# TensorE kept busy from the program's begin, one input piece on another queue, a third split sub-tile, and a new table of priority offsets

## The chip, the cores and the metric

One Trainium2 chip, eight cores, all running the same program on their own share of the data: core c works on half a stream of the prompt group (2048 rows of 1024 numbers) and on two short running streams (32 rows in all). TensorE is the matmul engine, VectorE (DVE), ScalarE (ACT) and GpSimd (POOL) do the element-wise work, and SyncE (SP), ScalarE and GpSimd each have a queue on which transfers are issued. The metric is the device time in microseconds (us) of one launch, taken from its slowest core.

## The reference

```python
def encoder_layer(x, ...):
    xn = rmsnorm(x, g_mix_pre)
    proj = xn @ w_in                       # 1024 -> 2048: [u | B | C | h]
    ...                                    # y_pool: trailing means of u, y_conv: gated conv of width 3
    merged = concat([group_rmsnorm(y_pool, ...), group_rmsnorm(y_conv, ...)])
    x = x + rmsnorm(merged @ w_out, g_mix_post)
    x = x + rmsnorm(cross_attn(rmsnorm(x, g_x_pre), mem_k, mem_v, w_q, w_co), g_x_post)
    hid = square(relu(rmsnorm(x, g_ff_pre) @ w_up))      # 1024 -> 4096
    x = x + rmsnorm(hid @ w_down, g_ff_post)
```

Three sub-layers, then: a mixer, attention into 256 memory rows, and an MLP with weights of 1024 x 4096. Each core also computes a share of the memory's keys and values, and the states that the streams carry on.

## The kernel before

The 2048 rows are four tiles of 512, each of four sub-tiles of 128 rows. `xT` holds a tile turned (features on partitions), `win`, `wout`, `up` and `wdn` hold weights as bf16, converted while they are loaded over GpSimd's queue. The stages run one after the other: the mixer of tiles 0 to 3, attention of tiles 2, 3, 0, 1, the MLP of tiles 0 to 3. Between the stages a tile goes to memory (`x1`, `x2`) and comes back.

The code only records operations, each with its engine, what it reads and writes, and an estimated cost. `Prog.schedule` then plays the program through with these estimates, and at each step an engine takes the ready operation with the lowest `prio`. What comes out is a fixed sequence per engine; in the run every engine executes its own in that order and waits with semaphores. `prio` is the place at which an operation was recorded, less an offset that the table `ORDER` gives for a named part and an engine. All matmuls have one line in the profile (L716), as do transposes (L721), ACT activations (L745) and transfers (L790).

The begin: tile 0 comes as four pieces `XT[0]` to `XT[3]` of 512 KB each, already turned, all on SP's queue. `pre_first` takes piece after piece: a square on ScalarE, two `scale_rows` that write `xT`, a sum on VectorE; the sum over partitions is one float32 matmul on `onesf`. ScalarE issues the load of `cst`, and then its first activation `warm`; the loads of w_in on GpSimd's queue wait for `warm` (`after=warm`). Behind them stand the rows of tile 1 and then w_out, one transfer of 4 MB read from memory, of which the first matmul `ps<-wout,mg` needs all.

`out_tile(t, ...)` is the product that closes a stage: per sub-tile two banks of PSUM (a pair) take nk chunks in two halves of 512 columns, and `post` then normalizes and adds. With `late=True` (MLP, tile 0) the first half of the chunks is done for two sub-tiles before the second half of `wdn` is asked for. There are four pairs in all.

Of the kernel before, what the change touches and what calls it, by code (L numbers as in the profile page):

```python
# [8 lines left out]
BF16 = mybir.dt.bfloat16  # L9
# [9 lines left out]
TN = 512  # L19
# [171 lines left out]
class Op:  # L191
# [2 lines left out]


ORDER = {
    ("conv_group 0", "dve"): -180, ("conv_group 12", "dve"): -70, ("conv_group 13", "act"): 340, ("conv_group 15", "dve"): 250,
    ("conv_group 6", "act"): -130, ("conv_group 7", "dve"): -50, ("ext_state_out 0", "pe"): -120, ("fin_conv 0", "dve"): -120,
# [6 lines left out]
    ("pool_group 14", "act"): 90, ("pool_group 6", "dve"): 60, ("post 10", "act"): 350, ("post 8", "dve"): -60,  # L205
    ("pre_sub 11", "act"): -30, ("pre_sub 12", "dve"): -10, ("pre_sub 13", "pe"): -120, ("pre_sub 2", "act"): 190,
# [4 lines left out]
}  # L211


class Prog:
# [72 lines left out]
    def schedule(self):  # L287
# [14 lines left out]
            if op.ndep == 0:  # L302
                release(op)

        free = {e: 2.0 if e == "pool" else 1.0 for e in self.ENGS}
        hold = {e: 0.0 for e in self.ENGS}
        bank_free = [0.0] * 8
        bank_busy = [None] * 8
# [70 lines left out]
        while left or any(dq.values()):  # L379
# [19 lines left out]
            now, e = best  # L399
# [21 lines left out]
            o, bk = pick  # L421
# [142 lines left out]
def build_program():  # L564
    nc = bass.Bass("TRN2", target_bir_lowering=False)
    BASE.clear()
    P = Prog(nc, n_dma_sems={"sp": 40, "pool": 24, "act": 4})
# [218 lines left out]
    def memset(ap, v, eng="dve"):  # L786
        P.add([(eng, lambda e, L: e.memset(ap, v), 0.3)], writes=[ap])
# [31 lines left out]
    warm = act(stat(128), epsb[:, 0:1], AF.Square)  # L819
    copy(idb[:, :], idf[:, :])  # L820

    def load_consts():
        memset(ones[:, :], 1.0)
        memset(onesf[:, :], 1.0)
        memset(onesr[:, :].bitcast(F32), 1.0)
        memset(bd64[:, :], 0.0)
        memset(bd64[0:64, 0:64], 1.0)
        memset(bd64[64:128, 64:128], 1.0)
        tt(pg[:, :], pv[:, 0:4], pv[:, 16:20], ALU.mult)

    def load_wpool():
        load(wpool[:, :], wpool_d[:, :], 262144, q="pool", after=warm)
# [106 lines left out]
    @named("pre_first")  # L939
    def pre_first():  # L940

        for i in range(4):
            x = XT[i]
            v = sqx[min(i, 1)][:, :]
            act(v, x, AF.Square)
            for c in range(2):
                kc = 2 * i + c
                scale_rows(xT[0][:, kc * TN:(kc + 1) * TN], x[:, c * TN:(c + 1) * TN], gcs[:, kc:kc + 1])
            if i > 0:
                tt(sqx[0][:, :], sqx[0][:, :], v, ALU.add)  # L950
        q = sqx[0][:, 0:TN]
        tt(q, q, sqx[0][:, TN:2 * TN], ALU.add)
        ps = PS(1)
        o2 = ps.v(0, 128, 0, TN)
        P.add([("pe", lambda e, L: e.matmul(L(o2), lhsT=onesf[:, :], rhs=q, start=True, stop=True, skip_group_check=True), 0.95)],
              reads=[onesf[:, :], q], writes=[o2])
        ln = rf[0][:, :]
        act(ln, o2, AF.Ln, scale=1.0 / D, bias=epsb[:, 0:1])
        act(r0[:, :], ln, AF.Exp, scale=-0.5)
        act(r0sq[:, :], ln, AF.Exp, scale=-1.0)  # L960

    def out_tile(t, chunks, nk, w, gp, dst, late=False):
# [10 lines left out]
                mm(ps.v(0, 128, h * 512, (h + 1) * 512), chunks(kc)[:, i * 128:(i + 1) * 128], w(kc, h),  # L973
                   kc == 0, kc == nk - 1)
        if late:
            for i in range(2):
                part(i, 0, nk // 2)
        for i in range(NSUB):
            part(i, nk // 2 if late and i < 2 else 0, nk)
            ps = tiles[i]  # L980
            X = Xof[(t, i)]
            row = t * TN + i * 128
            if dst is yp and t == NT - 1 and i == NSUB - 1:
                post_halves(ps, X, gp, yp[row:row + 128, :])
                continue
            post(ps, X, 128, gp, free_se=late_stage[0])
            if dst is None:
                continue
            dma("sp", dst[row:row + 128, :], X, 524288, wr=(dst is not yp))
# [494 lines left out]

    load_win(0, warm)
    for i in range(4):
        load(XT[i], xt0[i], 524288)
    load_consts()
    load_win(1, warm)
    load(Xe[0:NX, :], xe[:, :], NX * 4096, q="pool", after=warm)  # L1490
    load_wpool()
# [258 lines left out]
```

How the kernel before makes its waits and increments, by code:

```python
        def run(e, eng):  # L503
            seen = {}
            ends = sorted(dma_last.items(), key=lambda kv: kv[1].end)
            for n, op in enumerate(seqs[e]):
                if e == "sp" and n == len(seqs[e]) - 1:
                    for k, last in ends:
                        if last.end < op.start - SETTLED and seen.get(k, 0) < last.semval:
                            eng.wait_ge(dsem[k], last.semval)
                            seen[k] = last.semval
                waits = {}
                for p in plan[op]:
                    k, v = (p.sem, p.semval) if p.is_dma else (p.eng, p.sigval)
                    if seen.get(k, 0) >= v:
                        continue
                    if waits.get(k, 0) < v:
                        waits[k] = v
                for k, v in waits.items():
                    eng.wait_ge(dsem[k] if isinstance(k, tuple) else esem[k], v)
                    seen[k] = v
                ins = op.fn(eng, lambda x: x.resolve(psum) if isinstance(x, PV) else x)
                if op.is_dma:
                    ins.then_inc(dsem[op.sem], 16)
                elif op.needs_signal:
                    ins.then_inc(esem[e], 1)
            if e == "sp":
                for k, last in ends:
                    if seen.get(k, 0) < last.semval:
                        eng.wait_ge(dsem[k], last.semval)
```

## Time and profile before

| | |
|---|---|
| median of three runs | 840.95 us |
| fastest of them | 839.43 us |
| the profiled execution | 839.23 us |
| its span on the slowest core (core 3) | 837.7 us |
| spans of the eight cores | 834.6 to 837.7 us |
| TensorE busy in the span | 809.7 us (97%), 4529 matmuls |
| VectorE, ScalarE, GpSimd busy | 396.7, 386.4, 105.2 us |
| read from memory | 146.48 MB |

The span runs from the first to the last instruction of a core; 1.5 us of the profiled execution lie around it. A matmul of 512 columns is shown as 379 ns long at full clock, but its successor starts about 216 ns after it, since matmuls are pipelined.

### The profile page before, as it was taken

Reading aid. Unit: us, or ns where it says so; the run is one execution under the profiler, and the core shown is the slowest. Engines: PE = TensorE matmul, PEld = TensorE weight load, DVE = VectorE, ACT = ScalarE, POOL = GpSimd, SP = SyncE. Lnnn points to the kernel's source line nnn. Section 1 sums busy time; section 2 is a strip of 40 time slices with the busy share of each in tenths; the row PEclk is TensorE's granted clock in tenths of the full one; section 3 lists DMA queues with packets and bytes.
Section 4 is the critical chain, followed back from the end, with each engine's and each line's share of the span. In section 5 each row is a group of like instructions: output and inputs, shape, how many; then the busy total and the mean of one; then the engine's idle time right before and its main releaser. Section 6 shows DMA issues by size and latency. Waiting matters only on the chain.

```text
span 837.7 us, 13527 instructions; the slowest of 8 cores (834.6 to 837.7 us)
## 1 busy us (share of the span) xinstructions
PE 809.7 (97%) x4529; PEld 386.3 (46%) x4529; DVE 396.7 (47%) x552; ACT 386.4 (46%) x801; POOL 105.2 (13%) x182
## 2 busy tenths in 40 slices
PE   2889999999999999999999999999999999999997
PEld 1444445444564455454444454454444444444443
DVE  4797867689786676574231222232132322222112
ACT  4588756848775757674340323332133401233101
POOL 7523202130111104110010000000000000000000
PEclk9999999999999999999999999999999999999999
DMA  8999499430496526985799527861258810194011
GB/s 188 184 232 209 110 240 229 86 59 1 68 153 110 202 79 174 160 149 117 133 163 168 150 88 144 154 124 51 101 118 153 156 52 26 54 163 86 6 46 51
DMA packets 27120, 103.43 MB, mean 123 GB/s; under 512 B 2402, under 2 KB 9186, under 8 KB 21292
## 3 DMA queue, kind: packets, MB, share of 16 engines
q0 software_dynamic: 16736, 68.37, 47.4%
q1 hardware_dynamic: 10028, 33.80, 11.8%
q8 instruction: 38, 0.62, 0.3%
q10 hardware_dynamic: 288, 0.39, 0.2%
q14 instruction: 30, 0.25, 0.1%
HBM read 146.48 MB, written 18.07 MB: 196 GB/s over the span
## 4 chain that ended last, share of the span: by engine, by line
PE 85%; DMA 11%; issue 1%; POOL 1%; DVE 1%; ACT 1%; DVEq 0%; POOLq 0%; ACTq 0%
PE ps L716 83%; DMA wout<-w_out 6%; DMA wdn<-w_down 4%; PE ps L721 2%; DMA up<-w_up 1%; POOL win L790 0%; DVE mg L771 0%; DVE X L771 0%; POOL wdn L790 0%; DVE V L752 0%; ACT L745 0%; POOL X L790 0%; DVE xT L752 0%; POOL sT L790 0%; DVE z L752 0%
## 5 line engine op out<-in xcount | busy, mean ns | idle before, releaser
L716 PE MATMUL ps<-wdn,hid 128*128 128x512 bf16 x1024 | 222.3, 379 | 1.0 <-DMA wdn<-w_down 1.0
L716 PE MATMUL ps<-xT,up 128*128 128x512 bf16 x1024 | 222.8, 379 | 0.0
L716 PEld LDWEIGHTS ps<-wdn,hid 128*128 128x128 bf16 x1024 | 99.9, 98 | 120.5 <-issue 1.4
L716 PEld LDWEIGHTS ps<-xT,up 128*128 128x128 bf16 x1024 | 99.6, 98 | 119.6 <-issue 1.1
L752 DVE TENSOR_TENSOR O<-ps,gp 128x1024 f32<-128x1024 f32 (+1 forms) x49 | 58.7, 1200 | 184.5 <-PE ps L716 124.1
L745 ACT ACTIVATE rt<-ps 128x512 bf16<-128x512 f32 x128 | 76.4, 597 | 139.3 <-PE ps L716 133.3
L716 PE MATMUL ps<-xT,win 128*128 128x512 bf16 x512 | 124.4, 385 | 15.3 <-DMA win<-w_in 15.3
L752 DVE TENSOR_TENSOR hid<-rt 128x512 bf16<-128x512 bf16 x128 | 54.4, 425 | 150.8 <-ACT rt L745 148.9
L745 ACT ACTIVATE sqj<-ps 128x1024 bf16<-128x1024 f32 (+1 forms) x33 | 32.8, 994 | 175.8 <-PE ps L716 174.0
L716 PEld LDWEIGHTS ps<-xT,win 128*128 128x128 bf16 x512 | 49.9, 99 | 74.1 <-issue 19.2
L771 DVE SCALAR_TENSOR_TENSOR X<-O,st,X 128x1024 f32<-128x1024 f32 (+1 forms) x49 | 62.3, 1277 | 6.0 <-DVE O L752 5.4
L790 POOL DMA_DIRECT2D up<-w_up x32 | 17.2, 538 | 376.7 <-PE ps L716 357.6
L716 PE MATMUL ps<-wout,mg 128*128 128x512 bf16 x256 | 62.8, 379 | 0.8 <-DMA wout<-w_out 0.8
L716 PE MATMUL ps<-xT,Am 128*128 128x512 bf16 x256 | 58.2, 379 | 0.0
L716 PE MATMUL ps<-Bm,mg 128*128 128x512 bf16 x256 | 57.5, 379 | 0.0
L745 ACT ACTIVATE xs<-X 128x1024 bf16<-128x1024 f32 x40 | 42.1, 1053 | 32.9 <-DMA X<-x 25.0
L752 DVE TENSOR_TENSOR xT<-ps,cst 128x1024 bf16<-128x1024 bf16 x40 | 48.2, 1220 | 18.5 <-PE ps L721 18.4
L716 PEld LDWEIGHTS ps<-wout,mg 128*128 128x128 bf16 x256 | 24.8, 98 | 28.8 <-issue 1.6
L716 PEld LDWEIGHTS ps<-Bm,mg 128*128 128x128 bf16 x256 | 24.3, 98 | 28.4 <-issue 1.0
L716 PEld LDWEIGHTS ps<-xT,Am 128*128 128x128 bf16 x256 | 24.1, 98 | 28.3 <-issue 1.8
L754 POOL TENSOR_TENSOR psm<-mg 128x512 fp32r<-128x512 bf16 x16 | 19.2, 1198 | 94.8 <-ACT st L745 46.6
L745 ACT ACTIVATE rf<-ps,epsb 128x512 f32<-128x512 f32 x33 | 22.5, 682 | 15.6 <-PE ps L716 9.6
(203 smaller groups left out, 700.1 us busy)
## 6 DMA issues: line engine op xcount, KB each, us to landing
up<-w_up POOLq DMA_DIRECT2D x32, 1024.0 KB, 9.4
x<-X SPq DMA_DIRECT2D x16, 512.0 KB, 4.2
X<-x SPq DMA_DIRECT2D x16, 512.0 KB, 3.9
wdn<-w_down POOLq DMA_DIRECT2D x8, 1024.0 KB, 30.1
yp<-X SPq DMA_DIRECT2D x15, 512.0 KB, 2.6
X<-xp POOLq DMA_DIRECT2D x8, 512.0 KB, 44.0
X<-xp SPq DMA_DIRECT2D x8, 512.0 KB, 5.4
win<-w_in POOLq DMA_DIRECT2D x4, 768.0 KB, 25.5
```

The lines of the kernel that those rows point to most:

```text
L716: P.add([("pe", lambda e, L: e.matmul(L(out), lhsT=lhsT, rhs=rhs, start=start, stop=stop, skip_group_check=True), max(0.03, n * 0.000421 + ...
L721: P.add([("pe", lambda e, L: e.transpose(out=L(out), in_=in_, identity=idn), 0.065 if in_.dtype == BF16 else 0.25)], reads=[in_, idn], wri ...
L745: return e.activation(out=L(out), in_=L(in_), func=func, scale=scale, **kw)
L752: opts.append(("dve", lambda e, L: e.tensor_tensor(out=L(out), in0=L(in0), in1=L(in1), op=op), c_dve(n, per)))
L754: opts.append(("pool", lambda e, L: e.tensor_tensor(out=L(out), in0=L(in0), in1=L(in1), op=op), 0.18 + n * 0.00168))
L771: return P.add([("dve", lambda e, L: e.scalar_tensor_tensor(out=L(out), in0=L(in0), scalar=scalar, in1=L(in1), op0=op0, op1=op1), c_dve(nc ...
L790: return P.add([(q, lambda e, L: e.dma_start(out=out, in_=in_), 0.5 + nbytes / desc * 0.0005 if q == "pool" else 0.43)], reads=[in_] if rd ...
```

## The change

It has four parts. TensorE gets 34 matmuls whose result nobody reads (`spin`): 16 on a tile of ones, which need nothing but a memset, and 6 each after the first three pieces of tile 0 have been scaled. Piece 3 of tile 0 is loaded over ScalarE's queue, and the pieces are taken in the order 0, 3, 1, 2. The MLP's `out_tile` for tile 0 does the first half of three sub-tiles ahead, not of two. And `ORDER` has 67 offsets in place of 57, most of them other ones; with it the planner takes GpSimd to be free at 2.8, not 2.0.

```diff
@@ ORDER: all lines replaced; two of each
-    ("conv_group 0", "dve"): -180, ("conv_group 12", "dve"): -70, ("conv_group 13", "act"): 340, ("conv_group 15", "dve"): 250,
-    ("kv_block 0", "pe"): 40, ("kv_block 1", "act"): -280, ("kv_block 1", "pe"): -250, ("kv_block 3", "pe"): -60,
...
+    ("attn_head 1", "pe"): 620, ("attn_head 13", "pe"): 130, ("attn_head 14", "pe"): -250, ("conv_group 0", "dve"): -180,
+    ("group_rstd 7", "pe"): -30, ("kv_block 1", "pe"): -250, ("kv_block 3", "pe"): -60, ("out0_ 2", "pe"): -110,
...
-        free = {e: 2.0 if e == "pool" else 1.0 for e in self.ENGS}
+        free = {e: 2.8 if e == "pool" else 1.0 for e in self.ENGS}
...
+    busy = at("busy", hids.off + 2048, TN, BF16)
...
+        memset(busy[:, :], 1.0)
...
+    def spin(rhs, n, half):
+
+        o = PS(1).v(0, 128, 0, TN)
+        for _ in range(n):
+            P.add([("pe", lambda e, L: e.matmul(L(o), lhsT=ones[:, :], rhs=rhs, start=True, stop=True, skip_group_check=True),
+                    0.427 if half else 0.2133)], reads=[ones[:, :], rhs], writes=[o], lead=10 ** 6)
...
-        for i in range(4):
+        for j, i in enumerate((0, 3, 1, 2)):
             x = XT[i]
-            v = sqx[min(i, 1)][:, :]
+            v = sqx[min(j, 1)][:, :]
...
+            if j < 3:
+                spin(xT[0][:, 2 * i * TN:(2 * i + 1) * TN], 6, False)
...
         if late:
-            for i in range(2):
+            for i in range(3):
                 part(i, 0, nk // 2)
         for i in range(NSUB):
-            part(i, nk // 2 if late and i < 2 else 0, nk)
+            part(i, nk // 2 if late and i < 3 else 0, nk)
...
     for i in range(4):
-        load(XT[i], xt0[i], 524288)
+        load(XT[i], xt0[i], 524288, q="act" if i == 3 else "sp")
     load_consts()
+    spin(busy[:, :], 16, True)
```

ScalarE's sequence now opens with two transfers, `cst` and the piece, and then `warm`. Lines of the kernel's helpers move down a little: L716 becomes L718, L721 becomes L723.

What stands in a row, at three places. The first is TensorE's sequence around the first product with w_out (`wout,mg_80`: tile 0); `xs` are rows of tile 1 about to be turned, `xT_54` is tile 0 and `xT_55` tile 1. Before:

```order
L716 MATMUL ps<-xT_54,win 128x512 x24
L721 MATMUL ps<-idb,xs_59 128x128 x8
L721 MATMUL ps<-idb,xs_58 128x128 x8
L716 MATMUL ps<-sqe,bd_48 128x128
L721 MATMUL ps<-idb,xs_59 128x128 x8
L716 MATMUL ps<-wout,mg_80 128x512
L716 MATMUL ps<-sq_106,bd_48 128x512
L716 MATMUL ps<-wout,mg_80 128x512 x11
```

317 matmuls stand ahead of that first product. With the change:

```order
L718 MATMUL ps<-xT_54,win 128x512 x14
L718 MATMUL ps<-sqe,bd_48 128x128
L723 MATMUL ps<-idb,xs_59 128x128 x8
L723 MATMUL ps<-idb,xs_58 128x128 x8
L718 MATMUL ps<-wout,mg_80 128x512 x8
L718 MATMUL ps<-sq_106,bd_48 128x512
L718 MATMUL ps<-wout,mg_80 128x512 x7
L718 MATMUL ps<-xT_55,win 128x512 x23
```

351 matmuls stand ahead of it now, the same 317 in another order and the 34 of `spin`.

The second place is TensorE's sequence in the middle of the first stage, where rows of tile 2 (`xs0_58`, its second sub-tile) are turned between the products of tile 1 with w_out and of the memory with w_k. Before:

```order
L716 MATMUL ps1<-wout_91,mg1_81 128x512 x2
L716 MATMUL ps0<-wkv1_114,mT0_110 128x512
L716 MATMUL ps1<-wout_91,mg1_81 128x512
L716 MATMUL ps0<-wkv1_114,mT0_110 128x512
L716 MATMUL ps1<-wout_91,mg1_81 128x512
L721 MATMUL ps3<-idb_44,xs0_58 128x128 x8
L716 MATMUL ps0<-wkv1_114,mT0_110 128x512
```

With the change:

```order
L718 MATMUL ps0<-wout_91,mg1_81 128x512
L718 MATMUL ps3<-wkv1_114,mT0_110 128x512
L718 MATMUL ps0<-wout_91,mg1_81 128x512 x2
L723 MATMUL ps3<-idb_44,xs0_58 128x128 x8
L718 MATMUL ps0<-wout_91,mg1_81 128x512
L718 MATMUL ps2<-wkv1_114,mT0_110 128x512
```

660 matmuls stood ahead of these transposes, now it is 648 without those of `spin`. These rows come into the buffer that tile 0's second sub-tile leaves; its last w_out matmul was number 541, and is now number 506.

The third place is TensorE's sequence at the end of the MLP of tile 0: `wdn0` to `wdn3` are the first half of w_down, `wdn4` to `wdn7` the second. Before:

```order
L716 MATMUL ps2<-wdn2_142,hid1_132 128x512 x8
L716 MATMUL ps2<-wdn3_143,hid1_132 128x512 x8
L716 MATMUL ps1<-wdn4_144,hid2_133 128x512 x8
L716 MATMUL ps1<-wdn5_145,hid2_133 128x512 x8
L716 MATMUL ps1<-wdn6_146,hid3_134 128x512 x8
```

With the change:

```order
L718 MATMUL ps2<-wdn3_143,hid1_132 128x512 x8
L718 MATMUL ps1<-wdn0_140,hid0_131 128x512 x8
L718 MATMUL ps1<-wdn1_141,hid0_131 128x512 x8
L718 MATMUL ps1<-wdn2_142,hid1_132 128x512 x8
L718 MATMUL ps1<-wdn3_143,hid1_132 128x512 x8
L718 MATMUL ps0<-wdn4_144,hid2_133 128x512 x8
```

The 32 matmuls of the third sub-tile's first half have moved ahead of the first one that reads `wdn4`; the rest of the MLP keeps its order.

## Rows read from the trace of the kernel before

**Rows 1.** Cores 1, 3 and 7: span and mean granted TensorE clock.

```profile
core 1: 837.3 us, clock 0.999
...
core 3: 837.7 us, clock 0.999
...
core 7: 837.3 us, clock 1.000
```

**Rows 2.** Core 3 by stage: window, its length, busy time (instructions) of each engine, granted clock, DMA share, GB/s.

```profile
0.00:15.00 15.00, 0.00 (x0) 0.00 (x0) 5.87 (x16) 5.27 (x6) 11.52 (x26) 1.00 0.80 183
15.00:62.00 47.00, 42.20 (x322) 20.84 (x323) 37.83 (x78) 32.04 (x74) 18.82 (x43) 1.00 1.02 206
62.00:435.00 373.00, 371.35 (x2195) 181.61 (x2193) 253.73 (x310) 243.60 (x508) 63.27 (x92) 1.00 0.66 136
435.00:832.00 397.00, 396.05 (x2018) 183.86 (x2015) 97.13 (x146) 104.26 (x210) 11.64 (x22) 1.00 0.48 100
```

**Rows 3.** Core 3, who TensorE waited for: us in total, times, longest.

```profile
PE ps L716 <- DMA win<-w_in: 15.3, 1, 15.3
PE ps L716 <- ACT sq L745: 1.1, 2, 0.9
```

**Rows 4.** Core 3, TensorE in order of time, the first matmuls.

```profile
15.30 6.38 PE L716 MATMUL ps<-xT,win 128*128 128x512 bf16 x16 [15.30 <-DMA win<-w_in]
...
23.35 1.04 PE L716 MATMUL ps<-xT,win 128*128 128x512 bf16 x4
```

**Rows 5.** Core 3, the chain that ended last, in order of time.

```profile
11.73 49.27 DMA wout<-w_out
...
424.78 31.79 DMA wdn<-w_down
```

**Rows 6.** TensorE just before and at the first w_out matmul: cores 3, 1 and 7.

```profile
59.86 0.61 PE L721 MATMUL ps<-idb,xs 128*128 128x128 bf16 x8 [0.89 <-ACT xs L762]
61.24 0.38 PE L716 MATMUL ps<-wout,mg 128*128 128x512 bf16 x1 [0.77 <-DMA wout<-w_out]
...
60.95 0.38 PE L716 MATMUL ps<-wout,mg 128*128 128x512 bf16 x1 [1.17 <-DMA wout<-w_out]
...
60.70 0.38 PE L716 MATMUL ps<-wout,mg 128*128 128x512 bf16 x1
```

**Rows 7.** Core 3, the start of the DMAs: timeline, then DMA share and GB/s in windows.

```profile
1.07 0.41 ACTq L790 DMA_DIRECT2D cst<-consts  x1
...
2.87 0.20 ACT L745 ACTIVATE st<-epsb 128x1 f32<-128x1 f32 x1
3.68 1.21 POOL L790 DMA_DIRECT2D win<-w_in  x2 [2.98 <-ACT st L745]
...
5.00:6.00 1.00, 0.00 (x0) 0.00 (x0) 0.00 (x0) 0.00 (x0) 1.00 (x3) 1.00 0.65 128
6.00:7.00 1.00, 0.00 (x0) 0.00 (x0) 0.00 (x0) 0.00 (x0) 1.00 (x2) 1.00 0.86 199
```

**Rows 8.** Core 3, the second tile-2 transposes: the reload, the scaling, the matmuls.

```profile
120.92 1.06 ACT L745 ACTIVATE xs<-X 128x1024 bf16<-128x1024 f32 x1 [1.70 <-DMA X<-xp]
...
123.75 1.13 ACT L762 ACTIVATE xs<-X,st 128x1024 bf16<-128x1024 f32 x1
...
125.14 0.61 PE L721 MATMUL ps<-idb,xs 128*128 128x128 bf16 x8 [0.72 <-ACT st L745]
```

**Rows 9.** Core 3, around the matmuls on dg.

```profile
167.61 2.75 POOL L754 TENSOR_TENSOR dg<-idb,rb 128x1536 bf16<-128x1536 bf16 x1 [0.90 <-DVE rb L781]
167.97 2.93 DVE L771 SCALAR_TENSOR_TENSOR mg<-z,cst,rf 128x512 bf16<-128x512 f32 x1
...
171.65 0.81 PE L716 MATMUL ps<-dg,ones 128*128 128x512 bf16 x3 [0.73 <-DVE V L752]
```

**Rows 10.** TensorE at the second half of w_down: cores 3 and 7.

```profile
456.71 18.51 PE L716 MATMUL ps<-wdn,hid 128*128 128x512 bf16 x85 [0.95 <-DMA wdn<-w_down]
...
456.33 3.83 PE L716 MATMUL ps<-wdn,hid 128*128 128x512 bf16 x17 [1.24 <-DMA wdn<-w_down]
```

More of the change, by code:

```diff
@@ L196 @@
 ORDER = {
-    ("conv_group 0", "dve"): -180, ("conv_group 12", "dve"): -70, ("conv_group 13", "act"): 340, ("conv_group 15", "dve"): 250,
-    ("conv_group 6", "act"): -130, ("conv_group 7", "dve"): -50, ("ext_state_out 0", "pe"): -120, ("fin_conv 0", "dve"): -120,
[6 rows of a table removed]
-    ("pool_group 14", "act"): 90, ("pool_group 6", "dve"): 60, ("post 10", "act"): 350, ("post 8", "dve"): -60,
-    ("pre_sub 11", "act"): -30, ("pre_sub 12", "dve"): -10, ("pre_sub 13", "pe"): -120, ("pre_sub 2", "act"): 190,
[4 rows of a table removed]
+    ("attn_head 1", "pe"): 620, ("attn_head 13", "pe"): 130, ("attn_head 14", "pe"): -250, ("conv_group 0", "dve"): -180,
+    ("conv_group 1", "dve"): 30, ("conv_group 10", "act"): -170, ("conv_group 12", "dve"): 410, ("conv_group 4", "dve"): 60,
+    ("conv_group 6", "act"): 60, ("ext_conv 3", "dve"): 40, ("fin_attn 0", "pe"): -30, ("fin_attn 1", "act"): 60,
+    ("fin_attn 1", "pe"): 120, ("fin_attn 10", "act"): 180, ("fin_attn 11", "pe"): 60, ("fin_attn 12", "pe"): -110,
+    ("fin_attn 5", "act"): 50, ("fin_conv 0", "dve"): -240, ("fin_conv 1", "act"): -150, ("fin_conv 3", "act"): 240,
[5 rows of a table added]
+    ("pool_group 3", "dve"): -190, ("post 0", "act"): 460, ("post 0", "dve"): 460, ("pre_sub 1", "act"): 240,
[5 rows of a table added]
 }
@@ L948, in pre_first @@
                 scale_rows(xT[0][:, kc * TN:(kc + 1) * TN], x[:, c * TN:(c + 1) * TN], gcs[:, kc:kc + 1])
-            if i > 0:
+            if j < 3:
+                spin(xT[0][:, 2 * i * TN:(2 * i + 1) * TN], 6, False)
+            if j > 0:
                 tt(sqx[0][:, :], sqx[0][:, :], v, ALU.add)
```

18 rows, old and new, of the table ORDER are left out of this document.

## The prediction

> **What bounds the kernel now.** I read the cores first: the odd ones are the slow ones, 837.3 to 837.7 us, at a granted clock of 0.999 [rows 1]. Core 3, the slowest, carries the sum. Then the stages: TensorE is idle for 15.0 us until its first matmul, for 47.00 - 42.20 = 4.8 us until 62 us, for 373.00 - 371.35 = 1.65 us until 435 us and for 0.95 us until 832 us [rows 2]; then come the last normalization and store. From 62 us on it is the bound and nearly gap-free, so only its idle time and matmuls at half pace can be won. The waits put names to the first part: w_in 15.3 us, and 1.1 us for squares of ScalarE [rows 3].
>
> At the begin 16 matmuls take 6.38 us, some 400 ns from one to the next, and four later ones 1.04 us, some 217 ns apart [rows 4]; both spacings are 512 columns, at 1.2 and at 2.4 GHz. Before the first of them TensorE had done nothing. Less the last one's own 0.38 us, 15 steps took 6.0 us; at 216 ns they take 3.24. The half pace cost 2.8 us. That is what `spin` is about.
>
> The view that decides is the chain: from 11.73 us on, 49.27 us of it are the transfer of w_out, to 61.00 us [rows 5], and at 61.24 us TensorE, idle for 0.77 us, starts its first product with it; on core 1 it waited 1.17 us, on core 7 not at all [rows 6]. Meanwhile the DMA engines have no free time (share 1.02 from 15 to 62 us [rows 2]). Up to 61 us this program is bound by bytes, with TensorE just behind.
>
> **Part 1: the spin matmuls.** 16 start when `ones` and `busy` are set, about 2 us into the span, and even at 1.2 GHz they need 16 x 0.427 = 6.8 us: done by 9, six before the 15.3 us at which real work begins. The other 18 wait for scaled pieces and take 18 x 0.216 = 3.9 us at full pace; only those behind the third piece could delay anything, and w_in and the fourth piece are later. So they cost nothing on the path, the cover being the 15 us of waiting; without cover they would cost 10.7 us. Worth: up to 2.8 us by TensorE's clock. One extra memset on VectorE lies ahead of any data.
>
> **Part 2: piece 3 on ScalarE's queue.** It can start real work earlier. From 5 to 7 us the DMA engines stood at 0.65 and 0.86 [rows 7]: 0.35 + 0.14 = 0.5 us of transfer that a second queue can fill. It also has a price. ScalarE now issues two transfers ahead of `warm`, which ran at 2.87 us, and GpSimd's first load waits for `warm` until 3.68 us [rows 7]. One more issue like the first (0.41 us [rows 7]) moves all of GpSimd's queue by as much, w_out with it. So w_out lands between 0.5 us earlier and 0.4 us later; I take 0.1 us earlier.
>
> The Trainium skill's page "DMA: Bandwidth & Descriptors", under "Queues, rings and completion order", states that SP's and ScalarE's queues are rings on the same 16 DMA engines, which take turns between rings. By that rule the piece gets a larger share against GpSimd's loads, and no byte ahead of w_out disappears; the share of 1.02 agrees, and the sum stays as it is.
>
> **Parts 1 and 2 together, where it counts.** The order shows the same 317 real matmuls ahead of the first w_out product as before. If TensorE reaches this point 3 us or more earlier, it waits there for w_out: no other work has been put in front. So of 2.8 us and an earlier begin, what counts on core 3 is the 0.77 us of present wait plus the 0.1 us: 0.87 at the landing itself. But the last transposes before it waited 0.89 us for ScalarE's scaled rows [rows 6], and a part of what is behind w_out comes from the same queue of ScalarE; core 7, which did not wait for w_out, can gain less still. TensorE does not start at once when the transfer lands either (61.00 to 61.24). Ends: 1.3 us gained, 0.4 us lost. I take 0.5 us.
>
> **Part 3: the new order from 62 to 435 us.** In this stretch of core 3 there are 1.65 us of idle to win [rows 2], of which two waits are 0.72 us [rows 8] and 0.73 us [rows 9]. The first is TensorE waiting for rows of tile 2 that ScalarE had begun to square only at 120.92 us, after 1.70 us of waiting for their reload. With the change tile 0's second sub-tile finishes 541 - 506 = 35 matmuls earlier, some 35 x 0.216 = 7.6 us or less (transposes among them are shorter), and frees the buffer by as much; the transposes stand only 12 matmuls (2.6 us) earlier. This wait should go: 0.72 us. In the second, a VectorE operation took 2.93 us while GpSimd built `dg` in 2.75 us [rows 9]. GpSimd still builds `dg` just there, so VectorE is held up again; four matmuls of tile 2 now stand behind the `dg` matmuls and not ahead of them, which helps nothing. I leave that wait. New waits of the size of those present, one or two of 0.7 to 0.9 us, are as likely as anywhere in a new order. Ends: 1.65 us gained, 1.8 us lost. I take 0.6 us.
>
> **Part 4: the third split sub-tile.** TensorE waits 0.95 us for the second half of w_down, 1.24 us on core 7 [rows 10]; the transfers take 31.79 us from an issue that follows TensorE's own progress [rows 5], so an earlier or later TensorE brings the same wait. Now 32 matmuls, 32 x 0.216 = 6.9 us, are put ahead of it. They read weights and rows that are long there, and their pair of PSUM is free, since the fourth sub-tile, the small products and the next tile use the pairs in the same rhythm. The wait is covered seven times. The posts of the first two sub-tiles come 6.9 us later, to no harm: TensorE then has tile 1's products ahead of it for over 60 us. Worth 0.95 us, between 0.76 and 1.24 by core.
>
> **Sum.** 839.23 - 0.5 - 0.6 - 0.95 = 837.2 us, against the profiled execution. The median of the runs shown lies 1.7 us above that execution, the fastest 0.2 us; I go between: **838.0 us**.
>
> **Rivals.** First, **the begin passes through.** If w_out landed some microseconds earlier too, or its transfer were not what holds all cores, the 2.8 us of half pace and about 1.5 us of earlier begin would stay, with 0.6 and 0.95 us as above: 839.23 - 5.85 = 833.4 us, some 834 as a median. For it speaks core 7, where TensorE did not wait for w_out [rows 6]. Against it: there too the product began at 60.70 us, and the bytes ahead are the same. Chance 0.12.
>
> Second, **the second transposes of tile 2 wait longer.** They stand 12 matmuls earlier. If their rows came no earlier than now (reload landed at about 120.9 us, scaled by 124.88 us [rows 8]), TensorE would wait 0.72 + 2.6 = 3.3 us there in place of 0.72. The point that decides is whether the store and reload of that buffer go out with the earlier sub-tile or stay queued on SP behind another store. Then 839.23 - 0.5 - 0.95 + 2.6 = 840.4 us in the execution, 841.2 as a median, a little slower than before. Chance 0.15.
>
> Third, **nothing but w_down**: w_out lands 0.4 us later, the order's gains and losses cancel; 839.23 + 0.4 - 0.95 = 838.7 us, 839.5 as a median. Chance 0.2.
>
> Fourth, **a limiter on the clock.** In the rows the cores are granted 0.999 or 1.000 [rows 1] while all eight run dense matmuls; were TensorE's 809.7 busy us granted 13/16 instead, they would take 997 us. The Trainium skill, in "TensorE: Matmul & The Clock Gate" under "Seeing it yourself", states such a step to 13/16 once three cores of a die run dense matmuls, and that operands of ones don't trip it. By it the kernel before would have to show it already, and the trace disagrees. Chance 0.01.
>
> **How the numbers follow.** The forecast has 0.52. Its own bounds are 839.23 - 1.3 - 1.65 - 1.24 = 835.0 and 839.23 + 0.4 + 1.8 - 0.76 = 840.7 in the execution. The range must leave out no more than 2 in 10: down to 834.5, which cuts off most of the first rival, up to 841.5, which takes in the second and third. 2% of 841 us are 17 us, about what a measurement of this kernel can tell from no change; no case but the limiter comes near it, and idle time that could be won is about 15 us at the begin, which is bytes. Faster by over 2%: 0.01, slower: 0.01, within: 0.98.
>
> **What would show it.** In the changed kernel's profile the first matmuls should stand at about 2 us, and the first 16 on `win` some 216 ns apart (about 3.6 us together). TensorE should then wait for w_out for 2 us or more, landing at 60.5 to 61.4 us on core 3. The wait for w_down should be gone on all cores, that for tile 2's second sub-tile too, and the one at `dg` should remain. Wrong would be the forecast if w_out's wait stayed under 1 us with its product well before 60 us, or if a wait of over 1.5 us appeared between 62 and 435 us.

## The result, and the profile of the changed kernel

The changed kernel takes **846.51 us** (median of six executions, 846.16 to 847.87); the kernel before, timed beside it on the same chip, 841.56 us. The ratio is **1.0065, 95% interval 1.0046 to 1.0085**: 5.5 us slower (3.9 to 7.2), where 838.0 us, some 3 us faster, was forecast. Within 2% it is the same, as the chances had it; its sign and its size were wrong, and 846.5 lies outside the range of 834.5 to 841.5. The ratios here and below leave out executions in which the cores of one die ran slow at a lower granted clock (one of the kernel before took 1002.69 us at 0.816); medians beside them don't, so I go by ratios.

The profiled execution took 847.87 us. The cores first, as in [rows 1]: these are 4.3 to 8.6 us longer than before, and the fastest of the eight (841.6) is longer than the slowest was (837.7), so the loss is not that of one core.

```profile
core 1: 841.6 us, clock 0.999
...
core 3: 846.3 us, clock 0.995
...
core 7: 844.7 us, clock 0.996
```

The same stages of core 3 as in [rows 2]:

```profile
0.00:15.00 15.00, 9.48 (x30) 3.50 (x31) 5.47 (x18) 5.23 (x6) 11.04 (x24) 0.89 0.82 181
15.00:62.00 47.00, 41.46 (x333) 20.84 (x332) 40.16 (x80) 30.82 (x73) 22.05 (x47) 1.00 1.02 206
62.00:435.00 373.00, 369.51 (x2114) 177.94 (x2113) 252.06 (x308) 237.05 (x497) 64.32 (x90) 1.00 0.64 131
435.00:832.00 397.00, 397.00 (x2053) 184.89 (x2052) 99.07 (x152) 106.83 (x213) 12.58 (x24) 1.00 0.50 103
```

Read the instruction counts, not the busy time. From 62 to 435 us TensorE is idle for 3.5 us, 1.8 us more than before, but it got through 2114 matmuls in place of 2195 in the same 373 us; it was "busy" with fewer. The count is a sign and no size: 32 of the 81 are small ones that take 1 us together and now fall just behind 435 us. The size is read at one place of the program, the first product with w_down (before, then changed), both on core 3:

```profile
435.70 4.70 PE L716 MATMUL ps<-wdn,hid 128*128 128x512 bf16 x21
...
445.45 4.70 PE L718 MATMUL ps<-wdn,hid 128*128 128x512 bf16 x21
```

From the first product with w_out (61.24 before, 60.23 now) to this one TensorE took 374.5 us and now takes 385.2, 10.8 us more. A view of waits can't show most of that. What it does show, TensorE's waits on core 3 as in [rows 3] (total, times, longest), has one of 2.5 us, one of 0.4 us (`sq`, not shown) and three of 0.2 us in this stretch; what else is listed stands before 62 us:

```profile
PE ps L840 <- DVE xT L763: 3.5, 2, 2.6
PE ps L723 <- DVE xs L763: 2.5, 1, 2.5
...
PE ps L718 <- DVE z L754: 1.7, 2, 1.5
...
PE ps L718 <- DMA wout<-w_out: 0.6, 1, 0.6
```

**Where the time went: the groups of instructions.** TensorE's groups by line and shape (busy us, mean ns of one, idle before), the kernel before and then the changed one:

```profile
L716 PE MATMUL ps<-wco,mgs 128*32 128x256 bf16 x32 | 1.1, 274 | 0.0
```

```profile
L718 PE MATMUL ps<-wco,mgs 128*32 128x256 bf16 x32 | 6.7, 282 | 0.0
```

These are the 32 matmuls of `out_smp` in attention, which write 32 partitions each, four of them side by side. One by one they are no longer than before, 282 ns against 274, but together they fill 6.7 us and not 1.1. TensorE in order of time shows why. Before:

```profile
302.11 10.09 PE L716 MATMUL ps<-Bm,mg 128*128 128x512 bf16 x46
312.12 1.06 PE L716 MATMUL ps<-wco,mgs 128*32 128x256 bf16 x32
313.12 1.69 PE L716 MATMUL ps<-xT,Am 128*128 128x512 bf16 x7
```

With the change, the first rows of a stretch that goes on like this until 318.87 us:

```profile
306.67 0.28 PE L718 MATMUL ps<-wco,mgs 128*32 128x256 bf16 x1
306.88 0.39 PE L718 MATMUL ps<-Bm,mg 128*128 128x512 bf16 x1
307.20 0.28 PE L718 MATMUL ps<-wco,mgs 128*32 128x256 bf16 x1
307.42 0.39 PE L718 MATMUL ps<-Bm,mg 128*128 128x512 bf16 x1
307.74 0.28 PE L718 MATMUL ps<-wco,mgs 128*32 128x256 bf16 x1
...
318.55 0.39 PE L718 MATMUL ps<-wco,mgs 128*32 128x256 bf16 x5
318.87 1.47 PE L718 MATMUL ps<-Bm,mg 128*128 128x512 bf16 x6
```

In a row, the 32 take 313.12 - 312.12 = 1.00 us. Alternating with full-width matmuls they and 22 of those take 318.87 - 306.67 = 12.20 us; less 22 x 0.216 = 4.75, that leaves 7.45 us for the same 32. From a lone small one to the next start 0.21 us pass, and from the full one behind it to the next start 0.32, not 0.216. This costs **6.45 us**, and no row calls it a wait. Of the 10.8 us it is the largest part; 1.8 us are the added idle time, 1.7 us matmuls at half pace (below), and 0.8 us stay unassigned.

The single starts, which the rows above put together, say more. In the row of 32 four small ones start within 10 ns, and the next four some 110 ns after the first of them: these are the four side by side. Where a lone one stands between full ones, nothing starts beside it. One entry of the new table does it, `("out_smp 1", "pe"): 60`, which brings the 32 forward among the matmuls on `Bm`.

The Trainium skill, "TensorEngine Tiling (Array Packing)", under "Key Properties", says that changing the tiling mode drains TensorE. The rows agree so far that each change costs time, some 0.1 us on the way to the small ones (0.32 and not 0.216 us) and some 0.1 us on the way back (0.21 and not 0.11 us); whether TensorE drains in it they don't show.

**The begin**, TensorE in order of time, beside [rows 4]:

```profile
2.05 4.98 PE L840 MATMUL ps<-busy,ones 128*128 128x512 bf16 x16 [2.05 <-DVE onesf L789]
...
11.95 4.28 PE L840 MATMUL ps<-xT,ones 128*128 128x512 bf16 x12 [2.57 <-DVE xT L763]
16.07 3.62 PE L718 MATMUL ps<-xT,win 128*128 128x512 bf16 x16
```

The 16 products on `win` now take 3.62 us, not 6.38. They begin at 16.07 us, 0.8 us later than before, behind the last spin matmuls: on this core the clock had fallen during the 2.57 us without work, and some seven of these 12 ran at half pace (11 steps in 3.9 us, not 2.4). Averaged over the eight cores the first product on `win` starts at 15.2 us, before at 15.0: the real work does not begin earlier. **The first product with w_out**, on cores 3, 1 and 7, and w_out in the chain, beside [rows 5, 6]:

```profile
60.23 1.89 PE L718 MATMUL ps<-wout,mg 128*128 128x512 bf16 x8 [0.57 <-DMA wout<-w_out]
...
59.08 1.89 PE L718 MATMUL ps<-wout,mg 128*128 128x512 bf16 x8 [0.31 <-DMA wout<-w_out]
...
60.47 1.89 PE L718 MATMUL ps<-wout,mg 128*128 128x512 bf16 x8 [0.56 <-DMA wout<-w_out]
```

```profile
12.44 47.66 DMA wout<-w_out
```

It still gates all three, 0.2 to 1.9 us earlier than before. Most of that is not the change's: w_out was issued 0.7 us later than before (12.44, not 11.73) and landed, averaged over the cores, at 59.7 us, before at 59.6. What is new is that its first product starts 0.13 us after the landing and not, on average, 0.6. **Tile 2's second transposes**, beside [rows 8]: SP's issue of the reload before the change; then, changed, the chain, core 3 in order of time, and windows with the granted clock.

```profile
115.75 0.33 SPq L790 DMA_DIRECT2D X<-xp  x1
```

```profile
104.65 5.36 DMA x<-X
110.07 10.38 DMA X<-xp
```

```profile
120.54 1.06 ACT L747 ACTIVATE xs<-X 128x1024 bf16<-128x1024 f32 x1 [3.87 <-DMA X<-xp]
...
123.57 0.61 PE L723 MATMUL ps<-idb,xs 128*128 128x128 bf16 x8 [2.53 <-DVE xs L763]
```

```profile
124.00:126.00 2.00, 2.00 (x10) 0.81 (x8) 2.00 (x3) 1.29 (x4) 0.00 (x0) 0.58 0.90 219
126.00:128.00 2.00, 2.00 (x7) 0.70 (x5) 2.00 (x2) 0.05 (x1) 0.00 (x0) 0.57 1.02 404
```

The store of that buffer was issued at 104.65 us and the reload at 110.07, 5.7 us earlier than before; but the reload took 10.38 us, beside two more stores, and the rows were there at 120.5 us, as before (120.92). The wait grew from 0.72 to 2.53 us. After it, eight matmuls ran at 1.2 GHz (windows at a granted clock of 0.58 and 0.57), 8 x 0.21 = 1.7 us more, on this core alone. Cores 5, 6 and 7 wait for 1.4, 2.3 and 1.8 us before the next transposes of tile 2, at 128.8 to 133.8 us.

**The two other waits**, at `dg` beside [rows 9] and at w_down, cores 3 and 7, beside [rows 10]:

```profile
169.05 2.75 POOL L756 TENSOR_TENSOR dg<-idb,rb 128x1536 bf16<-128x1536 bf16 x1 [0.23 <-DVE rb L783]
...
172.73 0.81 PE L718 MATMUL ps<-dg,ones 128*128 128x512 bf16 x3
```

```profile
450.88 49.37 PE L718 MATMUL ps<-wdn,hid 128*128 128x512 bf16 x228
...
449.30 50.88 PE L718 MATMUL ps<-wdn,hid 128*128 128x512 bf16 x235
```

Neither has a wait any more: `dg` stood ready at 171.80 us, 0.9 us before its matmuls. But a wait of 0.4 us for `sq` (ScalarE) has come up 7 us later, on every core.

### The profile page after: what moved, and what is told of

The parts are those of the page before. It is cut to its first block, busy times and chain, and to the rows that moved or that the text cites. A ratio compares the mean times of both kernels' runs of the same rounds, so it can differ in the third digit from the quotient of the medians.

```text
span 846.3 us, 13586 instructions; the slowest of 8 cores (841.6 to 846.3 us)
## 1 busy us (share of the span) xinstructions
PE 826.2 (98%) x4563; PEld 390.9 (46%) x4563; DVE 399.6 (47%) x559; ACT 382.1 (45%) x794; POOL 110.0 (13%) x183
## 4 chain that ended last, share of the span: by engine, by line
PE 89%; DMA 7%; POOL 1%; DVE 1%; ACT 1%; issue 0%; DVEq 0%; ACTq 0%; POOLq 0%; SPq 0%
PE ps L718 87%; DMA wout<-w_out 6%; PE ps L723 2%; DMA X<-xp 1%; DMA x<-X 1%; POOL win L792 0%; DVE X L773 0%; DVE O L754 0%; POOL X L792 0%; DVE z L754 0%; ACT L747 0%; POOL sT L792 0%; ACT st L747 0%; DVE xs L763 0%; ACT sqj L747 0%
## 5 line engine op out<-in xcount | busy, mean ns | idle before, releaser
L718 PE MATMUL ps<-xT,up 128*128 128x512 bf16 x1024 | 223.0, 379 | 0.0
L718 PE MATMUL ps<-wdn,hid 128*128 128x512 bf16 x1024 | 222.2, 379 | 0.0
L718 PEld LDWEIGHTS ps<-wdn,hid 128*128 128x128 bf16 x1024 | 99.9, 98 | 119.4
L718 PEld LDWEIGHTS ps<-xT,up 128*128 128x128 bf16 x1024 | 99.6, 98 | 119.5 <-issue 1.1
L718 PE MATMUL ps<-xT,win 128*128 128x512 bf16 x512 | 122.4, 379 | 2.6 <-DMA win<-w_in 1.6
L718 PEld LDWEIGHTS ps<-xT,win 128*128 128x128 bf16 x512 | 48.8, 98 | 60.5 <-issue 5.0
L718 PE MATMUL ps<-wout,mg 128*128 128x512 bf16 x256 | 64.5, 383 | 0.8 <-DMA wout<-w_out 0.6
L773 DVE SCALAR_TENSOR_TENSOR X<-O,st,X 128x1024 f32<-128x1024 f32 (+1 forms) x49 | 62.2, 1272 | 6.4 <-DVE O L754 5.6
L718 PE MATMUL ps<-Bm,mg 128*128 128x512 bf16 x256 | 62.0, 380 | 0.0
L718 PE MATMUL ps<-xT,Am 128*128 128x512 bf16 x256 | 59.3, 379 | 0.0
L718 PEld LDWEIGHTS ps<-wout,mg 128*128 128x128 bf16 x256 | 24.8, 99 | 29.8 <-issue 3.4
L718 PEld LDWEIGHTS ps<-Bm,mg 128*128 128x128 bf16 x256 | 24.2, 98 | 28.5 <-issue 1.5
L718 PEld LDWEIGHTS ps<-xT,Am 128*128 128x128 bf16 x256 | 24.2, 98 | 27.6 <-issue 1.6
L723 PE MATMUL ps<-idb,xs 128*128 128x128 bf16 (+1 forms) x364 | 28.9, 218 | 3.0 <-DVE xs L763 2.5
```

The source lines that it names most:

```text
L718: P.add([("pe", lambda e, L: e.matmul(L(out), lhsT=lhsT, rhs=rhs, start=start, stop=stop, skip_group_check=True), max(0.03, n * 0.000421 + ...
L723: P.add([("pe", lambda e, L: e.transpose(out=L(out), in_=in_, identity=idn), 0.065 if in_.dtype == BF16 else 0.25)], reads=[in_, idn], wri ...
L773: return P.add([("dve", lambda e, L: e.scalar_tensor_tensor(out=L(out), in0=L(in0), scalar=scalar, in1=L(in1), op0=op0, op1=op1), c_dve(nc ...
```

## Experiments

Where a run must not be replanned, the kernel carries the sequence of each engine as a written list, which the planner only plays through; then nothing but the named edit moves. All ratios are to the kernel before, timed in the same call on the same chip.

**The run of 32 made whole, and broken by itself.**

```diff
 e1: the changed kernel
-    ("out3_ 3", "pe"): -30, ("out_smp 1", "pe"): 60, ("pool_group 11", "dve"): -120,
+    ("out3_ 3", "pe"): -30, ("pool_group 11", "dve"): -120,
 e2: the kernel before
+    ("out_smp 1", "pe"): 60,
```

> The changed kernel without the one offset on out_smp 1; its 32 matmuls of 32 columns (wco, mgs) stand in one row again, and nothing else moves but two ACT operations there. Theory A (alternating these with full-width matmuls costs the time): 32 of them and 22 full ones took 12.2 us, so 7.45 us for the 32, against 1.00 us in one row before; the time falls by 6.4 us against the changed kernel, to 840.1 us, and is about 1.5 us below before (ratio 0.998). Rival B (the loss is in the first 130 us: the matmuls of spin and the longer wait at tile 2's transposes): the time stays at 846 us. The rows of the 32 would then fall from 6.7 us busy to 1.1 us and the time would not follow.

> The kernel before with that one offset alone. The 32 matmuls then alternate with full-width ones, as in the changed kernel. Theory A: 6.4 us more than before, 847.9 us, ratio 1.0077. Rival B: no change, 841.5 us. If both causes count, the sum of this and of the run in which the row is made whole tells it: the two differences should be equal and opposite.

Measured: e1 **1.0007** (0.9995 to 1.0018), e2 **1.0071** (1.0046 to 1.0096). The group of 32, in e1 and then in e2:

```profile
L718 PE MATMUL ps<-wco,mgs 128*32 128x256 bf16 x32 | 1.1, 274 | 0.0
```

```profile
L716 PE MATMUL ps<-wco,mgs 128*32 128x256 bf16 x32 | 6.5, 282 | 0.0
```

That one entry costs the kernel before 6.0 us (3.9 to 8.1), as much as the whole change did; Rival B falls. Taken from the changed kernel, it gives back 1.0065 - 1.0007, or 4.9 us. But e1 was expected at 0.998 and stood at 1.0007: some 2 us of the forecast gain were missing besides.

**Two parts alone.** e3 is the kernel before, its sequences kept, with the begin of the change; e4 has the third split.

```diff
 e3: ahead of the written sequences
+    PE: 34 spin matmuls, then the kernel before, word for word
+    ACT: cst, XT[3], warm, ...    SP: XT[0], XT[1], XT[2], ...
 e4
-            for i in range(2):
+            for i in range(3):
                 part(i, 0, nk // 2)
```

> The sequences of the kernel before, operation for operation, with only the begin of the change: 34 matmuls of spin at the head of TensorE's sequence, piece 3 on ScalarE's queue, the order 0, 3, 1, 2. Theory A (the begin brings what w_out lets through): the first matmul on w_out moves from 61.2 us to 60.2 us on core 3, and the time falls by 0.5 to 1.0 us, to 840.8 us (ratio 0.9991). Rival B (spin costs: heat, or traffic moved in time): 2 us or more above before. Rival C (the begin passes through to the end whole): 1.5 us below or more.

> The kernel before with the third sub-tile split in the MLP's tile 0 and nothing else. Theory A: the wait for the second half of w_down (0.95 us on core 3, 1.24 us on core 7) goes and nothing takes its place: 0.9 to 1.1 us below before, 840.6 us, ratio 0.9988. Rival: the wait is found again at the end of the four sub-tiles, or PSUM pairs run out and the evacuation is waited for: no change or up to 0.5 us more.

Measured: e3 **1.0007** (0.9993 to 1.0022), e4 **0.9987** (0.9974 to 1.0001). The split brought 1.1 us (-0.1 to 2.2), near what was expected, but not certain by the time alone; the trace shows the wait gone on all eight cores. w_down on core 7 of e4, one unbroken group:

```profile
441.12 50.88 PE L716 MATMUL ps<-wdn,hid 128*128 128x512 bf16 x235
```

The begin brought nothing that can be seen. In e3 the wait for w_down is still there on core 1:

```profile
456.93 36.42 PE L860 MATMUL ps<-wdn,hid 128*128 128x512 bf16 x168 [0.96 <-DMA wdn<-w_down]
```

**The changed kernel again, and its order without the begin.** e6 keeps e1's sequences, takes out the 34 matmuls and puts piece 3 back on SP's queue.

```diff
 e5: no edit
 e6: e1's written sequences, less the begin
-    PE: 34 spin matmuls
-    ACT: cst, XT[3], warm, ...
+    SP: XT[0], XT[1], XT[2], XT[3], ...    pieces taken in the order 0, 1, 2, 3
```

> The changed kernel as it is, beside the next three on one chip. Theory A (the broken run of 32-column matmuls, +6.4 us, is nearly all of it): ratio to before 1.006 to 1.007. The wait before the second transposes of tile 2, 2.53 us on core 3 in the first profile: if it belongs to the new order it is above 1.5 us on most cores again; if it follows how transfers happen to share the memory in an execution, some cores show 0.4 us and others 2.5, and not the same ones.

> The order of the changed kernel with the run of 32 made whole, operation for operation, and the third split; but without the begin: no matmuls of spin, all four pieces on SP's queue in the order 0 to 3. Against before, theory A (the begin brings nothing, as its run alone said at 1.0007; the third split brings 1.1 us; the new order from 62 to 435 us brings 0.7 us at dg and loses as much at tile 2's transposes): ratio 0.9985 to 0.999, 838.3 us. Rival B (the new order itself costs about 1 us beside the broken run, since all three parts together stood at 1.0007): 1.000 or above, 839.5 us. Rival C (the begin costs 1 us in this order): this one is 1 us or more faster than the version with the begin, 840.2 us.

Measured: e5 **1.0064** (1.0051 to 1.0078), e6 **0.9987** (0.9978 to 0.9996). The result holds in a second measurement. In e5 core 3, which waited for 2.53 us before the second transposes of tile 2, doesn't wait there at all; core 0 does for 2.45 us, where it was 0.67, and the eight cores span 0 to 2.45 us: not the same cores. So the wait goes with the execution and not with the core; what makes the reload late in one was not tried. e6 leaves the new order at nothing beside the split, and points to the begin for e1's missing 2 us, though e1 ran on another chip.

**The old order, mended.** Four waits at once; e8 has the begin on top.

```diff
 e7, e8
-    load(wout[:, :], wout_d[:, :], 4194304, q="pool", desc=16384)
+    load(wout[:, 0:4096], wout_d[:, 0:4096], 2097152, q="pool", desc=16384)
+    load(wout[:, 4096:8192], wout_d[:, 4096:8192], 2097152, q="pool", desc=16384)
@@ TensorE's written sequence
-    out0 sub-tile 0: h 0 kc 0..5, then h 1 kc 0..5
+    out0 sub-tile 0: kc 0 h 0, kc 0 h 1, kc 1 h 0, ...
+    the transposes of pre_sub 8: 5 places later;  the 3 matmuls on dg: 5 places later
@@ out_tile, late
-            for i in range(2):
+            for i in range(3):
```

> The order of the kernel before with the third split, w_out read in two transfers of half the columns each, the first 12 matmuls on it taken so that 8 need only the first half, the second transposes of tile 2 and the three matmuls on dg each 5 places later. No matmuls of spin. Theory A (the waits for w_out 0.77 us, at the transposes 0.72 us, at dg 0.73 us and for w_down 0.95 us are real and nothing stands behind them): 2.5 to 3.2 us below before, ratio 0.9965. Rival (each is taken up by the next wait, for ACT or DVE, or by the next transfer): 1.0 us below, the third split alone, ratio 0.9988.

> The version before this one with the begin of the change added (34 matmuls of spin, piece 3 on ScalarE's queue, order 0, 3, 1, 2). Theory A (w_out held the begin back, and with w_out in halves the gain comes through): 1.0 to 2.0 us faster than that version, ratio to before 0.995. Rival (behind w_out stand waits for ACT and DVE that take the gain up, and in some cores the clock falls after such a wait): the same time as without the begin, within 0.5 us.

Measured: e7 **0.9965** (0.9953 to 0.9977), e8 **0.9972** (0.9960 to 0.9985). e7 is 2.9 us faster than the kernel before and some 8 us faster than the changed one on the same chip. Core 3 of e7 in order of time has no wait at the three places:

```profile
59.20 0.38 PE L863 MATMUL ps<-wout,mg 128*128 128x512 bf16 x1
...
123.76 0.61 PE L868 MATMUL ps<-idb,xs 128*128 128x128 bf16 x8
...
170.00 0.81 PE L863 MATMUL ps<-dg,ones 128*128 128x512 bf16 x3
```

Little stood behind them (0.3 us for `kn` on every core). How much of the 2.9 us each of the four waits gave was not tried, but for the split. The begin again added nothing, even with w_out in halves: its Theory A falls.

**Which half of the begin, and the transposes.** e9 is e1 with one edit, e10 and e11 are e6 with one each.

```diff
 e9: e1, TensorE's written sequence
+    the 8 transposes of pre_sub 8: 12 places later
 e10: e6, TensorE's written sequence
+    34 spin matmuls, then as in e6
 e11: e6
-        load(XT[i], xt0[i], 524288)
+        load(XT[i], xt0[i], 524288, q="act" if i == 3 else "sp")
     and the pieces taken in the order 0, 3, 1, 2
```

> The changed kernel with the run of 32 made whole, and the second transposes of tile 2 standing 12 matmuls later on TensorE, where the kernel before had them; nothing else. Theory A (the wait there is the reload's landing against the place of the transposes): 12 matmuls of 216 ns are 2.6 us, so the wait, 0.4 to 2.8 us by core in the changed kernel's traces, is nearly gone on all cores, and the time is about 1 us below the 1.0007 of the version with the transposes in their place: 0.9995. Rival (the matmuls that follow wait for these transposes, or the next reload gates instead): the wait shows again within 30 us, no change from 1.0007.

> The version with the new order and the third split alone (0.9987), and the 34 matmuls of spin ahead; all four pieces stay on SP's queue in the order 0 to 3. With the whole begin the same order stood at 1.0007, 0.2% or 1.7 us above. Theory A (spin costs it: the matmuls end late and a pause after them drops the clock in some cores): 1.0005 or above. Rival (the piece on ScalarE's queue costs it): 0.9985 or below, since the first 12 products with w_in then run at full clock.

> The same version (new order, third split) with piece 3 on ScalarE's queue and the order 0, 3, 1, 2, and no matmuls of spin. Theory A (spin costs the 0.2%): 0.9987, as without either. Rival (the queue move costs it): 1.0005 or above. If both this and the run with spin alone stand near 0.9987, the 0.2% was the spread of two chips.

Measured: e9 **0.9976** (0.9961 to 0.9991), e10 **0.9966** (0.9946 to 0.9985), e11 **0.9984** (0.9965 to 1.0003). Read them with care. This was a third chip, and on it cores 4 to 7 set the time: in the kernel before they took 842.4 us on average, cores 0 to 3 took 836.3. In stretches TensorE was granted less there. Core 4 of e9:

```profile
352.50:366.50 14.00, 14.00 (x63) 6.48 (x63) 6.96 (x8) 9.34 (x18) 3.46 (x3) 0.81 1.03 169
```

By the slowest of cores 0 to 3 alone the ratios are 0.9994 (e9), 1.0003 (e10) and 0.9995 (e11), each uncertain by up to 0.0009. So neither half of the begin shows a cost of 0.2%, and Theory A of e10 isn't borne out; but with spin alone it stands above the version with the queue move alone, and which half costs what stays open. Nor is e9's 0.9976 a gain by the later transposes. So the begin and the place of the transposes were set two by two on the chip of e5 to e8: e13 is e1 again, e14 is e6, e15 is e9, and the last is new.

```diff
 e16: e6, TensorE's written sequence
+    the 8 transposes of pre_sub 8: 12 places later
```

> Four versions of the new order with the run of 32 made whole, beside each other on one chip: with or without the begin, the second transposes of tile 2 where the change has them (early) or 12 matmuls later. This one: with the begin, early. It stood at 1.0007 of before. Theory A (begin and early transposes work against each other: a TensorE that comes sooner waits longer for the reload): this one is the slowest of the four by 1.5 to 2.5 us. Rival (1.0007 was the spread between chips): all four within 0.1%, near 0.998.

> Without the begin, early transposes. It stood at 0.9987. Theory A: 0.998 to 0.999, 1.0 us below the one with the begin. Rival: the same as with it.

> With the begin, transposes 12 matmuls later. It stood at 0.9976. Theory A: 0.9975, 2 us or more below the version with the begin and early transposes. Rival: within 0.1% of it.

> Without the begin, transposes 12 matmuls later. Theory A: without a wait at the reload the begin's gain (up to 1 us before w_out) is seen, so this one is 0.5 to 1 us above the one with the begin, 0.9985. Rival: the begin brings nothing even then, 0.9975.

| ratio to before | transposes early | 12 later |
|---|---|---|
| with the begin | e13: 1.0003 (0.9992 to 1.0015) | e15: 0.9996 (0.9983 to 1.0009) |
| without | e14: 0.9995 (0.9977 to 1.0012) | e16: 0.9988 (0.9977 to 0.9998) |

The early transposes cost 0.0007 in either row, the begin 0.0008 in either column: 0.6 us each, none of it certain by itself. The same kernels measured twice differ by as much and more: e1 and e13 1.0007 and 1.0003, e6 and e14 (one chip) 0.9987 and 0.9995, e9 and e15 0.9976 and 0.9996. Theory A's 2 us don't show, nor does any gain by the begin; nor do the four lie within 0.1% near 0.998, as the rival had it.

The whole begin was tried in four such pairs (e3, e8 against e7, e13, e15), and each time the version with it was 0.0007 or 0.0008 slower. The mean of the eight cores' spans, which varies less than the slowest core, is longer with it in all four too, by 0.2, 0.5, 0.4 and 0.6 us. For the early transposes that mean gives nothing (0.0 and 0.2 us). Moving the second transposes has its own price: in e9, e15 and e16 every core waits 0.6 us for `kn` soon after.

The traces show where the begin's gain goes, in one execution each. w_out lands at 60.6 to 60.9 us in all four, averaged over the eight cores. Its first product starts 0.1 us later with the begin (61.0 in e13, 60.7 in e15), 0.7 and 0.5 us later without (61.5 in e14, 61.2 in e16): 0.5 us gained. From there to the last matmul the means are 771.7 and 770.4 us with it, 770.4 and 770.4 without: with early transposes (e13) it is more than given back. With late ones it should have stayed by these traces, but the time of e15 is no better than that of e16; why is open. The transposes on core 1 of e13 and of e14:

```profile
123.91 0.77 PE L723 MATMUL ps<-idb,xs 128*128 128x128 bf16 x8 [2.16 <-DVE xs L763]
```

```profile
124.36 0.61 PE L866 MATMUL ps<-idb,xs 128*128 128x128 bf16 x8 [1.35 <-DVE xs L906]
```

After the longer wait the clock fell on this core too. Windows of core 1 of e13:

```profile
124.00:126.00 2.00, 2.00 (x12) 1.09 (x12) 2.00 (x2) 1.63 (x6) 0.00 (x0) 0.55 0.80 219
126.00:128.00 2.00, 2.00 (x7) 0.72 (x6) 2.00 (x3) 0.61 (x1) 0.00 (x0) 0.59 0.89 283
```

**The price of one break.** e7 with the 32 in four groups of 8.

```diff
@@ TensorE's written sequence
-    Bm x6, wco,mgs x32
+    wco,mgs x8, Bm x2, wco,mgs x8, Bm x2, wco,mgs x8, Bm x2, wco,mgs x8
```

> The mended old order (0.9965) with the run of 32 matmuls of 32 columns parted into four of 8, two full-width ones between each; a look at the trace. Theory A (each further change from a full matmul to a run of these and back costs the same; 21 further ones cost 6.4 us, so 0.31 us each): three further ones cost 0.9 us. Rival (the cost is by the matmul, 0.2 us for each of the 32 that has a full one near it): 6 us, as in the changed kernel.

One execution, 842.75 us, and its trace. Core 3 in order of time:

```profile
310.58 0.40 PE L864 MATMUL ps<-wco,mgs 128*32 128x256 bf16 x8
310.92 0.60 PE L864 MATMUL ps<-Bm,mg 128*128 128x512 bf16 x2
311.45 0.40 PE L864 MATMUL ps<-wco,mgs 128*32 128x256 bf16 x8
...
313.19 0.40 PE L864 MATMUL ps<-wco,mgs 128*32 128x256 bf16 x8
313.52 1.68 PE L864 MATMUL ps<-xT,Am 128*128 128x512 bf16 x7
```

The stretch takes 2.94 us; less 6 x 0.216, 1.64 us are left for the 32, against 1.00: three more breaks cost 0.64 us, 0.21 each. The cost goes by the break and not by the matmul, as Theory A said, but a group of 8 pays less than a lone one: the changed kernel has 23 groups, so 22 further breaks (the expectation counted 21), and 6.45 / 22 = 0.29. The starts account for the difference: a group of 8 still goes in fours, while a lone one takes the 0.11 us of four for itself and not a quarter of it, 0.08 us more.

## Why the prediction was wrong, by its own steps

**Parts 1 and 2, the begin: the gate right, the worth not.** Spin matmuls at 2.05 us, full pace on `win` and w_out as the gate came as foretold. "So they cost nothing on the path" did not hold: on core 3 twelve of them stood in front of the first real product, which began 0.8 us late. The price of Part 2 came (w_out was issued 0.7 us later, where 0.4 was put down), but its mean landing moved by 0.1 us only. "TensorE should then wait for w_out for 2 us or more" did not come. It waited 0.57 us on core 3, because the real work had not begun earlier, and work ahead of it waited for VectorE (`z`, 1.5 us). The term was 0.5 us of gain (1.3 to -0.4). At w_out 0.5 us is what the two by two shows. At the end it was -0.6 us in four pairs, each uncertain by more. The step that failed is that what counts at w_out counts at the end. In e13 it is given back at the reload of tile 2, the next transfer that TensorE meets, which doesn't come earlier; that this is so in general is not shown (e15).

**Part 3, the new order: here the prediction failed.** It read the stretch from 62 to 435 us for idle time only, "there are 1.65 us of idle to win", and gave its upper bound, 1.8 us of loss, as the sum of new waits. The size of matmuls and the company they are in had no term. The new sequence of TensorE has `Bm,mg` and `wco,mgs 32x256` alternating for 45 rows, in plain sight, and the trace of before had the price of the row that was to be broken (32 in 1.00 us). 6.0 us (e2), 6.45 us in the trace, were missing from the sum; with them alone it would have been 838.0 + 6.0 = 844.0 us. The stated bounds for this part were 1.65 us gained and 1.8 us lost; the cost left out is over three times the larger. Nor did the 0.6 us of gain come: the new order with its run whole stands at nothing.

"This wait should go: 0.72 us", said of tile 2's second transposes, was wrong too. It was the second rival's mechanism: the buffer came free and the reload went out 5.7 us earlier, but it landed when it had, and TensorE stood there 12 matmuls sooner. The rival's price was 2.6 us more; it is 0.6 us at most on the time, and uncertain (e13 against e15, e14 against e16), though single cores lose up to 4.2 us there, half-pace matmuls included. Its deciding point, a store ahead on SP's queue, did not occur as put; the reload was issued early and took 10.38 us. What slowed it, the two stores beside it or the other transfers, was not tried. And the `dg` wait of 0.73 us, which "should remain", went, with 0.4 us for `sq` in its place. The new order without its two faults equals the old: e16, 0.9988, and e4, 0.9987.

**Part 4, the third split: right in its mechanism.** The wait is gone on all cores. 0.95 us was the term, 1.1 us (-0.1 to 2.2) the measurement, which can't tell it from nothing.

**The sum.** In ratios: the split -0.0013, the new order 0, its early transposes +0.0007, the begin +0.0008, the broken run +0.0071, together +0.0073 or 6.1 us; measured were 1.0065 and 1.0064, within the intervals. That the small terms add up so well is in part luck, since each is within its noise; only the broken run is clear of it. With the run whole, two chips gave 1.0007 and 1.0003. The limiter on the clock, the fourth rival, has no part in this: the mean granted clock was 0.995 or more on every core in the changed kernel's six executions. But "the trace disagrees" held for one trace and not for all: on the chip of e9 to e12 the kernel before was granted 0.990 on cores 4 to 7 on average, and e9's trace has 0.81 (13/16) there in stretches. The begin brings nothing; that it costs some tenths of a us is likely, how much is open.

## What to carry to other kernels

When an order of instructions changes, don't look at waits alone: count what TensorE gets through in a stretch, and look in the new order for small matmuls that used to stand in a row and now alternate with full ones. A planner that prices each such matmul at a fixed share of its columns, as this one does at a third, sees no difference; it must price the change between the two kinds. And a gain ahead of a transfer that gates is worth only what the next gate lets through: here mending four waits brought 2.9 us, starting TensorE 13 us earlier with work that nobody reads nothing.

## What the runs showed of the hardware

- Matmuls that write 32 partitions, four beside each other, start four at a time, every 0.11 us, while they stand in a row (32 in 1.00 us); a lone one takes 0.21 us if a full-width matmul follows, and the full one ahead of the next then takes 0.32 us instead of 0.216. Going over and back cost 0.29 us for a lone one and 0.21 us for a group of 8. TensorE does not show as idle in it.
- After TensorE had stood without work for 2.0 to 2.6 us, the granted clock fell to its lower level, 1.2 GHz (0.55 to 0.6 as the mean of a window), on some cores and not on others: it fell on core 3 of the changed kernel (2.53 us), core 1 of e13 (2.16) and core 1 of e5 (2.03), about 1.7 us lost in the first; it did not on core 0 of e5 (2.45) and core 6 of the changed kernel (2.34).
- The granted clock in the views doesn't show the half pace of the first matmuls: [rows 2] has 1.00 from 15 to 62 us, where [rows 4] has 16 of them some 400 ns apart. Read the spacing.
- All eight cores ran dense matmuls at a granted clock of 0.995 or more in the changed kernel's profile; core 4 of e9 was granted 0.81 from 352.5 to 366.5 us.
- The time at which the same transfer, w_out, lands differs between cores of one execution by up to 3.1 us (e15: 59.1 to 62.2 us), and the cores that come last are others in the next run. One core's wait in one profile is a weak price for an edit.
